# Second feed-forward product of an encoder layer by Strassen's scheme, its output by tokens

## What is computed

```python
h2 = modulate(rmsnorm(x, norm_mlp_g[l]), shift2, scale2)
y = jnp.square(jax.nn.relu(h2 @ w_ff1[l])) @ w_ff2[l]
x = x + gate2 * y
```

## Time and profile before

| | us |
|---|---|
| median of 3 runs | 2383.65 (2382.06 to 2384.64) |
| profiled execution, its own time | 2379.64 |
| its span, first to last instruction | 2377.7 |
| PE busy | 2288.2 (96%), 10448 matmuls |
| DVE busy | 934.4 (39%) |
| ACT busy | 716.1 (30%) |
| POOL busy | 948.0 (40%) |
| mean granted TensorE clock | 0.979 of full speed |

### The profile page before, as it was taken

How to read it: one execution, slowest core, us unless ns; L and a number is a source line. 1 busy time by engine, 2 the same in 40 slices (tenths; PEclk the granted TensorE clock), 3 DMA queues, 4 the chain that set the end, 5 groups by cost and what they waited for, 6 DMA issues and landing times.

```text
span 2377.7 us, 26865 instructions
## 1 busy us (share of the span) xinstructions
PE 2288.2 (96%) x10448; PEld 1909.9 (80%) x10448; DVE 934.4 (39%) x1188; ACT 716.1 (30%) x980; POOL 948.0 (40%) x438
## 2 busy tenths in 40 slices
PE   3789999999998999999999999999999999999999
...
PEclk6889999999999999999999999999999999999999
...
GB/s 337 311 244 171 135 164 173 169 183 220 246 225 208 196 265 160 134 246 168 98 90 105 97 97 95 95 95 96 96 97 97 94 100 97 97 97 97 97 107 80
DMA packets 188698, 355.44 MB, mean 149 GB/s; under 512 B 13258, under 2 KB 40396, under 8 KB 187344
## 3 DMA queue, kind: packets, MB, share of 16 engines
...
## 4 chain that ended last, share of the span: by engine, by line
PE 86%; DVE 7%; issue 2%; DMA 2%; ACT 1%; SPq 1%; POOL 0%; ACTq 0%; DVEq 0%; POOLq 0%
PE ps L698 27%; PE ps L700 27%; PE ps L699 27%; DVE acc L1656 2%; PE ps L732 1%; DMA araw<-in_w_ada 1%; DVE accx L1780 1%; PE ps L937 1%; DVE rt L1921 1%; DMA gb<-g_d 1%; DVE yc L1828 0%; DMA o_d<-yc 0%; DVE utmp L1671 0%; PE ps L1100 0%; DVE gw L1881 0%
## 5 line engine op out<-in xcount | busy, mean ns | idle before, releaser
L313 POOL TENSOR_TENSOR wlo<-wraw,whi 128x1024 fp32r<-128x1024 f32 (+2 forms) x372 | 914.1, 2462 | 1213.5 <-ACT whi L308 1205.5
L308 ACT ACTIVATE whi<-wraw 128x1024 fp32r<-128x1024 f32 x376 | 391.3, 1046 | 1187.6 <-PE ps L700 1161.6
L698 PE MATMUL ps<-h2T,whi 128*128 128x512 f32 x1024 | 399.6, 390 | 2.5 <-DVE h2T L2189 2.5
L699 PE MATMUL ps<-h2T,whi 128*128 128x512 f32 x1024 | 399.3, 390 | 0.0
L700 PE MATMUL ps<-h2T,wlo 128*128 128x512 f32 x1024 | 399.2, 390 | 0.0
L698 PE MATMUL ps<-ah,whi 128*128 128x512 f32 x1024 | 399.2, 390 | 0.0
L700 PE MATMUL ps<-ah,wlo 128*128 128x512 f32 x1024 | 398.7, 389 | 0.0
L699 PE MATMUL ps<-al,whi 128*128 128x512 f32 x1024 | 398.6, 389 | 0.0
L2214 DVE TENSOR_TENSOR sq<-utmp 128x512 f32<-128x512 f32 x64 | 71.9, 1142 | 560.3 <-ACT utmp L1594 549.9
L2236 DVE SCALAR_TENSOR_TENSOR x1T<-ps,M,x1T 128x512 f32<-128x512 f32 x128 | 87.5, 744 | 515.4 <-PE ps L700 515.4
L698 PEld LDWEIGHTS ps<-h2T,whi 128*128 128x128 f32 x1024 | 192.8, 188 | 43.9 <-issue 4.0
...
## 6 DMA issues: line engine op xcount, KB each, us to landing
wraw<-in_w_ff SPq DMA_DIRECT2D x256, 512.0 KB, 3.6
araw<-in_w_ada SPq DMA_DIRECT2D x128, 512.0 KB, 5.3
wraw<-in_w_in SPq DMA_DIRECT2D x72, 512.0 KB, 5.9
arawx<-in_w_ada SPq DMA_DIRECT2D x64, 512.0 KB, 4.6
wraw<-in_w_out SPq DMA_DIRECT2D x32, 512.0 KB, 5.8
xnat<-in_x ACTq DMA_DIRECT2D x4, 1024.0 KB, 7.9
...
qk_d<-sth ACTq DMA_DIRECT2D x16, 256.0 KB, 2.6
```

Source lines behind the costliest of these rows:

```text
L308: act.activation(whi[:, slot, 0:kb, 0:cols], wraw[:, slot, 0:kb, 0:cols], ACT.Copy).then_inc(hi_ready, 1)
L313: pool.tensor_tensor(wlo[:, slot, 0:kb, 0:cols], wraw[:, slot, 0:kb, 0:cols], whi[:, slot, 0:kb, 0:cols].bitcast(F), ALU.subtract).then_in ...
L698: pe.matmul(dst, lhs[0], rhs[0], start=start, stop=False)
L699: pe.matmul(dst, lhs[0], rhs[1], start=False, stop=False)
```

## The change

The hidden features are cut into 16 chunks of 512. In 15 of them the second product, 512 tokens x 512 hidden times 512 hidden x 2048, is made by Strassen's scheme in Winograd's form. A chunk gives two halves h (output columns j and j + 2 of four groups of 512). In a half, activations A and weights B are cut in two by two quarters; B's quarters are the tiles `wq` 0 to 3. Seven products of half size replace eight: each is 256 tokens x 256 hidden times 256 hidden x 512, 12 matmuls of 128x512, so 84 a half where 96 stood. Three of the weight operands are quarters as loaded (split by ACT and POOL as before); four are sums that DVE forms (`form`), ACT rounds, and DVE again subtracts into low parts (`formed_lo`). Four sums of activations are also made on DVE (`act_sum`), and each of the seven activation operands is rounded by ACT (`act_hi`) and gets its low part on DVE (`act_lo`). Products accumulate in PSUM where the scheme allows; after each one DVE adds two banks onto `yacc`, by tokens (`add_product`).

Between the products of a half stand four blocks of the first product of a later chunk (`half_order`). Banks 0 to 3 serve the first product, 4 and 5 or 6 and 7 the Strassen products in turn: product number G waits till number G - 2 is added. The last chunk (blocks "V") is done plainly, by tokens. Loops are written out. The 32 steps for `gate2` move from the first chunk to two in each of the first 16 halves, from a single buffer `araw3`. `x1T` is stored to HBM at the start, loaded back into the place of `h2T` at the end, transposed (64 transposes as before), and the last steps on DVE multiply by `gate2` and add.

Matmuls of the stage by the order of PE's instructions: 3072 for the first product, 2520 for 210 Strassen products, 192 for the last chunk, 5784 in all.

The core of the diff:

```diff
-CH = 1024
+CH = 512
 CHUNKS = DFF // CH
 CT = CH // P
-CB = CH // 512 * GB + G_OUT * (CT // KB)
+HALVES = 2 * (CHUNKS - 1)
+RAW_FF1 = GB * CHUNKS
+G2_STEPS = 32
...
+PRODUCTS = 7
+ON_X = (0, 2, 4, 6)
+FORMED = (1, 2, 4, 6)
+QUADRANT = ((0, 0), (1, 1), (0, 1), (0, 1), (1, 1), (0, 0), (1, 0))
+FIRST_IN = (0, 1, 2, 6)
+WEIGHTS_AT = {0: 0, 2: 0, 3: 2, 4: 1, 5: 3}
+def ff1_of(h):
+    c = h // 2
+    if h % 2 == 0:
+        return [("F", c + 1, b) for b in range(4, 8)]
+    if c + 2 < CHUNKS:
+        return [("F", c + 2, b) for b in range(4)]
+    return [("V", 0, 0), ("V", 0, 1)]
+def half_order(h):
+    w = [("W", h, k) for k in range(PRODUCTS)]
+    f = ff1_of(h)
+    if len(f) == 2:
+        return w[:4] + f[:1] + w[4:6] + f[1:] + w[6:]
+    return w[:2] + f[:1] + w[2:4] + f[1:2] + w[4:6] + f[2:3] + w[6:] + f[3:]
...
+        def quarter_load(h, r):
+            if h == 0:
+                sp.wait_ge(ada_step, 160)
+            elif r == 0:
+                sp.wait_ge(t_formed, 4 * h)
+            elif r == 1:
+                sp.wait_ge(t_lo, 4 * (h - 1) + 3)
+            elif r == 2:
+                sp.wait_ge(t_formed, 4 * (h - 1) + 3)
+                sp.wait_ge(lo_ready, LO_AT["W", h - 1, 3])
+            else:
+                sp.wait_ge(t_formed, 4 * h)
+                sp.wait_ge(lo_ready, LO_AT["W", h - 1, 5])
+            c, j = h // 2, h % 2
+            k, s = ((0, 0), (0, 1), (1, 1), (1, 0))[r]
+            kt, f = CT * c + KB * k, 512 * (j + 2 * s)
+            sp.dma_start(wq[:, r, :, :], w_ff23[:, kt:kt + KB, f:f + 512]).then_inc(wq_loaded[r], 16)
...
+        def gate2_load(s):
+            if s < G2_STEPS:
+                sp.wait_ge(ada_step, 160 + s)
+                sp.dma_start(araw3[:, :, :], w_ada3[:, s % 16, 10 * 1024 + 1024 * (s // 16):
+                                                    11 * 1024 + 1024 * (s // 16)]
+                             .rearrange("p (w n) -> p w n", w=2)).then_inc(ada_loaded[4], 16)
...
-        with pool.Fori(1, CB * CHUNKS // 4) as i:
-            for s in range(4):
-                split_lo(pool, N_FF + 4 * i + s, s)
+        for key in POOL_ORDER[4:]:
+            n = FF_AT[key]
+            slot = n % RING
+            pool.wait_ge(hi_ready, n + 1)
+            if key[0] == "W":
+                raw = wq[:, WEIGHTS_AT[key[2]], :, :]
+            else:
+                raw = wraw[:, raw_place(key) % RING, :, :]
+            pool.tensor_tensor(wlo[:, slot, :, :], raw, whi[:, slot, :, :].bitcast(F), ALU.subtract
+                               ).then_inc(lo_ready, 1)
...
+        def ff2_block(h, k):
+            n = FF_AT["W", h, k]
+            c, j, G = h // 2, h % 2, PRODUCTS * h + k
+            on_x = k in ON_X
+            bank = 4 if on_x == (j == 0) else 6
+            if k in FORMED:
+                pe.wait_ge(t_lo, 4 * h + FORMED.index(k) + 1)
+            else:
+                pe.wait_ge(lo_ready, LO_AT["W", h, k])
+            pe.wait_ge(f_lo, PRODUCTS * c + k + 1)
+            if G >= 2:
+                pe.wait_ge(f_added, G - 1)
+            for m in range(2):
+                for i in range(KB):
+                    a = [t[:, k, i, m * P:(m + 1) * P] for t in (ahi, alo)]
+                    w = [t[:, n % RING, i, :] for t in (whi, wlo)]
+                    new = k in (0, 1, 5) and i == 0
+                    dst = ps[:, bank + m, :]
+                    pe.matmul(dst, a[0], w[0], start=new, stop=False, skip_group_check=True)
+                    pe.matmul(dst, a[0], w[1], start=False, stop=False, skip_group_check=True)
+                    ins = pe.matmul(dst, a[1], w[0], start=False, stop=i == KB - 1, skip_group_check=True)
+            ins.then_inc(blk_done, 1)
...
+        def relu(c):
+            base = 0 if c else 4
+            act.wait_ge(blk_done, FF_AT["F", c, GB - 1] + 1)
+            for i in range(CT):
+                if 4 * c + i >= 2:
+                    act.wait_ge(f_sq, 4 * c + i - 1)
+                act.activation(rutmp[:, i % 2, :], ps[:, base + i, :], ACT.Relu).then_inc(f_relu, 1)
+        def act_hi(c, o):
+            if o in (1, 2, 3, 4):
+                act.wait_ge(f_sum, 4 * c + o)
+                src = asum[:, o, :, :]
+            else:
+                act.wait_ge(f_sq, 4 * c + (2 if o == 0 else 4))
+                src = rawa[:, 0 if o == 0 else 2:2 if o == 0 else 4, 256 if o == 6 else 0:512 if o == 6 else 256]
+            if c:
+                act.wait_ge(blk_done, FF_AT["W", 2 * c - 1, o] + 1)
+            act.activation(ahi[:, o, :, :], src, ACT.Copy).then_inc(f_hi, 1)
...
+        def squares(c):
+            base = 0 if c else 4
+            for i in range(CT):
+                dve.wait_ge(f_relu, 4 * c + i + 1)
+                dve.tensor_tensor(rawa[:, i, :], ps[:, base + i, :], rutmp[:, i % 2, :], ALU.mult
+                                  ).then_inc(f_sq, 1)
...
+        a11, a12 = rawa[:, 0:2, 0:256], rawa[:, 2:4, 0:256]
+        a21, a22 = rawa[:, 0:2, 256:512], rawa[:, 2:4, 256:512]
+        def act_sum(c, o):
+            if c:
+                dve.wait_ge(blk_done, FF_AT["W", 2 * c - 1, o] + 1)
+            if o == 1:
+                dve.wait_ge(f_sq, 4 * c + 4)
+            elif o in (2, 3):
+                dve.wait_ge(f_sum, 4 * c + o - 1)
+            a, b, op = {1: (a21, a22, ALU.add), 2: (asum[:, 1, :, :], a11, ALU.subtract),
+                        3: (a12, asum[:, 2, :, :], ALU.subtract), 4: (a11, a21, ALU.subtract)}[o]
+            dve.tensor_tensor(asum[:, o, :, :], a, b, op).then_inc(f_sum, 1)
+        def act_lo(c, o):
+            dve.wait_ge(f_hi, PRODUCTS * c + o + 1)
+            src = {0: a11, 5: a12, 6: a22}[o] if o in (0, 5, 6) else asum[:, o, :, :]
+            dve.tensor_tensor(alo[:, o, :, :], src, ahi[:, o, :, :].bitcast(F), ALU.subtract).then_inc(f_lo, 1)
+        def form(h, k):
+            n = FF_AT["W", h, k]
+            slot = n % RING
+            b11, b12, b22, b21 = [wq[:, r, :, :] for r in range(4)]
+            if k == 1:
+                for r in (0, 1):
+                    dve.wait_ge(wq_loaded[r], 16 * (h + 1))
+                dve.wait_ge(blk_done, n - RING + 1)
+                ins = dve.tensor_tensor(tlo[:, slot, :, :], b12, b11, ALU.subtract)
+            elif k == 4:
+                dve.wait_ge(wq_loaded[2], 16 * (h + 1))
+                dve.wait_ge(t_formed, 4 * h + 1)
+                ins = dve.tensor_tensor(b12, b22, b12, ALU.subtract)
+            elif k == 2:
+                dve.wait_ge(t_formed, 4 * h + 2)
+                dve.wait_ge(lo_ready, LO_AT["W", h, 0])
+                ins = dve.tensor_tensor(b11, b12, b11, ALU.add)
+            else:
+                dve.wait_ge(wq_loaded[3], 16 * (h + 1))
+                dve.wait_ge(t_formed, 4 * h + 3)
+                dve.wait_ge(blk_done, n - RING + 1)
+                ins = dve.tensor_tensor(tlo[:, slot, :, :], b21, b11, ALU.subtract)
+            ins.then_inc(t_formed, 1)
+        def formed_lo(h, k):
+            n = FF_AT["W", h, k]
+            slot = n % RING
+            dve.wait_ge(hi_ready, n + 1)
+            raw = wq[:, WEIGHTS_AT[k], :, :] if k in WEIGHTS_AT else tlo[:, slot, :, :]
+            dve.tensor_tensor(wlo[:, slot, :, :], raw, whi[:, slot, :, :].bitcast(F), ALU.subtract
+                              ).then_inc(t_lo, 1)
+        def add_product(h, k):
+            c, j, G = h // 2, h % 2, PRODUCTS * h + k
+            bank = 4 if (k in ON_X) == (j == 0) else 6
+            r, s = QUADRANT[k]
+            f = 512 * (j + 2 * s)
+            y = yacc[:, 2 * r:2 * r + 2, f:f + 512]
+            dve.wait_ge(blk_done, FF_AT["W", h, k] + 1)
+            if G == 0:
+                dve.wait_ge(xT_stored, 32)
+            if c == 0 and k in FIRST_IN:
+                ins = dve.tensor_copy(y, ps[:, bank:bank + 2, :])
+            else:
+                dve.wait_ge(f_added, G)
+                ins = dve.tensor_tensor(y, ps[:, bank:bank + 2, :], y, ALU.add)
+            ins.then_inc(f_added, 1)
...
+        for h in range(HALVES):
+            c, odd, last = h // 2, h % 2, h == HALVES - 1
+            gen = odd and not last
+            if odd:
+                squares(c + 1)
+            formed_lo(h, 2)
+            add_product(h, 0)
+            if not odd and c:
+                act_lo(c, 6)
+            if last:
+                for kt in range(CT):
+                    dve.wait_ge(f_hi, PRODUCTS * (c + 1) + kt + 1)
+                    dve.tensor_tensor(vl[:, kt, :], rawa[:, kt, :], vh[:, kt, :].bitcast(F), ALU.subtract
+                                      ).then_inc(f_lo, 1)
+            add_product(h, 1)
+            if h in (9, 17):
+                m = M_G2 + 8 * (h == 17)
+                ada_cols(10 if h == 9 else 11, 3, m, m + 4)
+            if gen:
+                act_sum(c + 1, 1)
+                act_lo(c + 1, 0)
+            gate2_step(2 * h)
+            formed_lo(h, 4)
+            add_product(h, 2)
+            if gen:
+                act_sum(c + 1, 2)
```

(114 more changed lines are left out.)

377 lines of the change are left out of this document (198 added, 179 removed).

## The result

| | before | changed |
|---|---|---|
| median of 4 runs, us | 2383.56 (2382.06 to 2384.64) | 2317.31 (2316.59 to 2319.63) |
| span of the profiled execution | 2377.7 | 2314.9 |
| first to last matmul of the feed-forward stage | 1404.3 | 1341.6 |

The ratio is 0.9724, 95% interval 0.9707 to 0.9741: 2.8% faster. Forecast were 2309.4 us and a range of 2302 to 2340. The profiled executions differ by 62.8 us of span, and the stage alone by 62.8: nothing came from elsewhere.

A forecast was written before the change was run, and what follows sets the result against it. PE's number of matmuls was taken to bound the stage. -81.5 + 2 + 2.5 + 2.5 + 0.3 = -74.2 us takes the profiled 2379.64 to 2305.4; the median stands 4.0 higher, 2309.4, range 2302 to 2340.

The forecast's parts named there:

- What bounds the kernel: Feed-forward stage: PE's number of matmuls sets the time; 6144 become 5784 at 0.2265 us each, saving 81.5 us.
- Starts of blocks: Feed-forward stage: PE's starts of blocks, with up to three semaphores each, cost between 0 and 6 us; taken as 0.
- DVE beside PE: Strassen halves: DVE, held up at times while POOL splits (a meeting), needs 39.0 of PE's 40.8 us in odd halves.
- The deadline of product 6: Product 6's formed weight has 10.9 us; one meeting with POOL fits, two are 0.9 late; stage loss 2 us.
- rival 1: Product 6's formed weight comes late in most halves, with two meetings with POOL, giving 2323 to 2340 us; chance 0.16.
- Rival 2: POOL goes first at each of its splits during DVE's chain to product 6, giving 2433 us, slower; chance 0.05.
- Rival 3: PE's rate suffers, from starts of blocks or late transfers, over 0.03 us a start; 0.2 each gives 2351 us; chance 0.04.
- Last half: Last Strassen half: steps on ACT and DVE come late for PE, which loses 2.5 us, bounds 1.5 to 5.
- End, third group: After the last Strassen product: DVE's addition and last steps delay PE's third group by 0.1 to 4.1 us, taken as 2.5.
- Very end: After PE's last work: DVE ends 2.4 us later, then the store; 5.3 us against 5.05 before, so 0.3 more.
- Transfers, the first four blocks, `gate2` loads: Weight transfers cost 0; four blocks before the first Strassen product cover DVE's work, 0, at worst 2; `gate2` steps already counted.
- The signs: New profile: PE waits under 10 us, nearly all in the last 80; wrong if a half's mean matmul step exceeds 0.23.

## Why the prediction was right, point by point

- **What bounds the kernel.** PE's count of matmuls, before and after. Right: 81.4 us for 360 matmuls, measured by putting them back; 81.5 forecast. By the 216 ns that the Trainium skill (VectorE: DVE Perf Modes, section on the TRN2 errata) gives for a matmul of 512 columns, an estimate would be 77.8; the measurement decides for 0.2267 us.
- **Starts of blocks.** Taken at 0. From 1768 to 2176 PE lost 1.0 us over some 110 starts (0.20 in each of five odd halves, behind product 6; the even halves took 40.80 us each). Right.
- **DVE beside PE.** 39.0 us in an odd half was the estimate, 8.4 of it for meetings; measured are 38.7, 9.8 of it meetings. In the even half the estimate was 21.6 with no meeting; measured are 29.4, 8.3 of it meetings. That was missed. Half 14 still lost nothing, so it cost no time.
- **The deadline of product 6.** Right as a mechanism, and the term that was mis-sized. The prediction has "with one meeting 9.8, with two 11.8, 0.9 late", and then "for the whole stage I take 2 us, with bounds 0 and 15". The price of one case was right: in half 13 the chain took 11.9 us from the freed tile (1597.82) to the low part (1609.71), where 11.8 stood for two meetings. How often it would happen was not. The trace has two meetings in each of the 14 odd halves before the last, 1.36 us lost in each of the first eight and 0.20 in the six others: 8 x 1.36 + 6 x 0.20 = 12.1 us. The prediction gives no sum for its 2 us. I had treated meetings as chance, with an average of half a split; they are fixed by the order, and repeat in each half. So rival 1 came true in the eight halves with `gate2` steps, and "in most halves" did not: without the step two meetings nearly fit.
- **Rival 2** (POOL first at each of its splits, 2433 us) did not happen. POOL had two splits in the window, not four: it waited 5.2 us for ACT in front of the first. Rival 3 (PE's rate) neither: 0.227 us a matmul.
- **Last half.** 2.5 us forecast; the two waits cost 1.45 and 1.26, 2.7 in all. Right, and for the reason given.
- **End, third group.** 2.5 forecast, 2.7 measured, through one meeting (4.29 us for 2.29).
- **Very end.** 0.3 forecast; from the last matmul's start to the end 5.36 us against 5.39, so 0. But eight transposes that stood behind the last matmul now stand before it, 0.9 us that the sum left out. The prediction also counts 52 transposes in the old stage where the trace has 56; that changes its 12.7 us of rest by 0.4 and no term.
- **Transfers, the first four blocks, `gate2` loads.** Taken at 0; PE waits for none of them.
- **The signs.** Two of the prediction's own signs went against it. PE's waits come to 13.1 us from 1034 us on, not under 10, and 8.3 of them lie before the last 80 us. And it calls itself wrong "if the mean step between matmuls in a half is over 0.23 us": it is 0.234 in the first eight odd halves (in one of them, half 9, 16 tiny matmuls for `gate2` stand besides). Both are the deadline term again. The waits on a formed weight stay under the 15 us that were the other limit, and the clock did not fall in the traced stage beyond its start (0.93 from 968 to 1000 us, 0.94 before).

The terms as measured, -81.4 + 12.1 + 2.7 + 2.7 + 0.9 = -63.0, against -62.8 for the stage; 0.2 us stays unassigned. The forecast was -74.2, so the miss is 11.4 us, and 10.1 of it is the deadline term. By the medians the miss is only 7.9 us, since the profiled execution of before lay 4.0 below its median and that of the changed kernel only 0.6. That is luck: the forecast's number looks better than its sum was.
